# 56 of 96 modulation tiles computed on VectorE as multiply-and-sum over rows, 40 left on TensorE

## The chip, the cores and the metric

The kernel runs on one core of one Trainium2 chip. The time is that of the device for one execution, in microseconds, and a version's time is the median of its runs. Four engines compute: TensorE (PE), VectorE (DVE), ScalarE (ACT) and GpSimd (POOL). SyncE (SP) issues all transfers from memory here, from one queue, in program order.

## The reference, cut to what matters

One latent stream of 256 tokens and a context of 256 tokens, 1024 features each, go through two layers (attention with low-rank queries and keys, then a state-space mixer), each followed by a SwiGLU FFN of width 2816. What the change touches is the modulation: each layer turns two vectors, `c` (latent tokens) and `c_ctx` (context tokens), into 6 x 1024 numbers each.

```python
for i in range(DEPTH):                        # DEPTH = 2
    mod     = silu(c)     @ ada_w[i] + ada_b[i]    # 1024 x 6144, latent
    mod_ctx = silu(c_ctx) @ ada_w[i] + ada_b[i]    # the same weights, context
    shift_a, scale_a, gate_a, shift_m, scale_m, gate_m = split(mod, 6)
    x = x + gate_a * mixer_i(rms_norm(x) * (1 + scale_a) + shift_a)
    x = x + gate_m * ffn_i(rms_norm(x) * (1 + scale_m) + shift_m)
```

So 2 x 6144 output features, each a dot product of length 1024 with either vector. In tiles of 128 output features that is 96 tiles of 128 x 1024 weights, 48 for a layer, 8 for each of the six parts. All of it is float32.

## The kernel before, in words

Tokens lie along the free dimension: 512 for the first layer (256 context, 256 latent), features on partitions. Every large product is made to float32 accuracy from three matmuls on a weight block of 128 x 128: the weights are split into a high part (ACT copies `raw` into `w_hi`, line 537) and a low part (DVE subtracts, line 879), and lines 1324 to 1326 multiply low x high, high x high and high x low. A **weight tile** is 128 x 1024 (eight blocks, 24 matmuls). Four `raw`, `w_hi` and `w_lo` buffers form a ring: tile n+4 can be split once PE is done with tile n. A tile's number starts with `WO` (output projection), `F0` (FFN w1 and w3) or `G0` (FFN w2).

The first FFN runs 22 **rounds** `j`: PE multiplies tile `F0+2j` (w1) and `F0+2j+1` (w3), 48 matmuls over 512 tokens. ACT takes the SiLU of the first product (line 723), splits the next two weight tiles' high parts, and copies the hidden tile's high part (line 727). DVE makes, in this order, the low part of one weight tile, the product of the two halves (line 1090), the low part of the other weight tile, and the low part of the hidden tile (line 1093). Then `w2` runs eight steps `m` of three weight tiles (66 matmuls); PE waits ahead of them for all 22 hidden tiles (`hid_lo`). DVE adds each finished step to the residual with the gate (line 1068), ACT squares it, and POOL sums the squares for the next norm.

The modulation tiles are spread over the program. 16 are multiplied at the start, 32 in the 16 attention heads (two a head) and 48 in the first FFN (two a round, four left over in the first two steps of w2). For a tile, PE runs 8 matmuls of 32 x 128 outputs (line 1359, function `ada`), with the two SiLU vectors as the stationary operand; four of them stand side by side in the array. After four tiles DVE copies the sum out (line 941), PE transposes it back (line 1378, `turn`), and DVE adds the bias (line 946). In the program's order `ada_two` stands behind the FFN round's 48 matmuls, and in a head between the transposes of the probabilities and the next head's scores. PE executes its queue in order, so a modulation tile that has not landed holds up all that follows. The tiles land in two halves of `scratch` (T), by SP's line 281, after SP has issued the weight tiles of the round two later.

Of the kernel before, what the change touches and what calls it, by code (L numbers as in the profile page):

```python
# [76 lines left out]
ADA1 = ADA0 + 2 * HEADS  # L77
# [30 lines left out]
SHARED = (0, 3, 4, 5, 6)  # L108
ODD = [sum(NORM_K[v] // 2 for v in range(w) if v in SHARED) for w in range(len(NORM_K) + 1)]
# [12 lines left out]
def program(nc, a, out):  # L122
# [9 lines left out]
    with ExitStack() as fixed:  # L132
# [103 lines left out]
        ada_used = sem("ada_used")  # L236
        row_cp, row_tr, mod_ev, mod_done = sem("row_copied"), sem("row_turned"), sem("mod_out"), sem("mod_done")
# [30 lines left out]
        def _(sp):  # L268
# [46 lines left out]
            queries(1, 0)  # L315
            sp.wait_ge(nlo, NB[3])
            with sp.Fori(0, 7) as j:
                for u in range(2):
                    queries(2 * j + u + 2, 1 - u)
                    ada_head(2 * j + u)  # L320
            for t in range(8):
                load(WO + t, WO + t, 1024, one("w_o", t))
                if t in (1, 3):
                    ada_head(14 + t // 2)
# [12 lines left out]
            with sp.Fori(1, KH // 2) as i:  # L337
# [5 lines left out]
            for m in range(8):  # L343
                for r, (k0, k1) in enumerate(K3):
                    load(g0(m) + r, g0(m) + r, 128 * (k1 - k0), one("w2", m)[:, 128 * k0:128 * k1])
                    if 3 * m + r in (1, 3, 5, 8):
                        two(KH - 2 + (1, 3, 5, 8).index(3 * m + r))
# [27 lines left out]
        def _(pool):  # L375
# [4 lines left out]
            def accumulate(w, n):  # L380
# [3 lines left out]
                for k in range(1, NORM_K[w] - 1):  # L384
# [3 lines left out]
                    before = T[:, b % 2, 0:n] if k == 1 else T[:, 6, 0:n]  # L388
                    nc.gpsimd.tensor_tensor(T[:, 6, 0:n], before, T[:, (b + k) % 2, 0:n], ADD).then_inc(sq_used, 2 if k == 1 else 1)  # L389
# [45 lines left out]
            pool.wait_ge(ada_used, 96)  # L435
# [90 lines left out]
        def _(act):  # L526
# [184 lines left out]
            head(15, 7, 1)  # L711
            for m in range(8):
# [157 lines left out]
        def _(dve):  # L870
# [78 lines left out]
            def gains(which, layer, chunk, name, groups, k):  # L949

                dve.wait_ge(mod_ev, groups)
# [16 lines left out]
            gains(0, 0, 1, "norm_mix", 4, 1)  # L968
# [57 lines left out]
            def head(i, j, u):  # L1026
# [4 lines left out]
                if u:  # L1031
# [8 lines left out]
                if u:  # L1040
# [19 lines left out]
            gains(1, 0, 4, "norm_ffn", 12, 2)  # L1060
# [18 lines left out]
            def hidden(j, g, u, nt, Uh, Ul, n, s, group=None):  # L1079

                if group is not None:
                    ada_rows(group, 4 * group + 4, bank[7])
                lo(n + 4, s + 4)
                if group is not None:
                    ada_out(group, 1, group - 12)
# [10 lines left out]
            for j in range(2):  # L1096
                hidden(j, j, j % 2, TOK, U0h, U0l, F0 + 2 * j, F0 + 2 * j)
            with dve.Fori(1, KH // 2) as i:
                for u in range(2):
                    hidden(2 * i + u, 2 * i + u, u, TOK, U0h, U0l, F0 + 4 * i + 2 * u, F0 + 2 * u, None if u else 11 + i)  # L1100
            for m in range(8):
                group = {0: 22, 2: 23}.get(m)
                if group:
                    ada_rows(group, 4 * group + 4, bank[7])
                for n in range(g0(m), g0(m + 1)):
                    if n == g0(m) + 2:
                        add(g0(m) + 3, m, m % 2, 0, 5, both)
                    lo(n + RING, n + RING)
                    if n == g0(m) + 1 and group:
                        ada_out(group, 1, group - 12)  # L1110
                if m == 2:
                    gains(2, 1, 1, "norm_mix", 24, 3)
                    gains(3, 1, 4, "norm_ffn", 24, 4)
# [205 lines left out]
        def _(pe):  # L1319
# [8 lines left out]
            def tile(n, s, o, h, l, k0, nk, first, final, mid=None):  # L1328

                pe.wait_ge(w_lo, n + 1)  # L1330
                for k in range(nk):
# [3 lines left out]
                    if k == 3 and mid is not None:  # L1335
                        mid()
# [516 lines left out]
```

## Time and profile before

| | us |
|---|---|
| median of 3 runs | 1361.28 (1359.84 to 1369.13) |
| profiled execution, its own time | 1365.47 |
| its span, first to last instruction | 1363.5 |
| PE busy | 1238.5 (91%) |
| DVE busy | 712.3 (52%) |
| ACT busy | 581.1 (43%) |
| POOL busy | 232.8 (17%) |

PE is busy for most of the span. The mean granted TensorE clock is 0.964 of full speed. The engines' shares are means over stages that differ: start, attention heads (about 112 to 296 us), output projection (to 343), first FFN (353 to 768), state-space mixer, and second FFN, whose tiles carry 256 tokens.

### The profile page before, as it was taken

How to read it: one execution, taken by the hardware profiler on the slowest of the kernel's cores; microseconds unless marked ns; L12 is line 12 of the kernel's file. 1: busy time of each engine (PE TensorE's matmuls, PEld its weight loads, DVE VectorE, ACT ScalarE, POOL GpSimd, SP SyncE). 2: the span in 40 equal slices, each digit the busy share in tenths (PEclk: the TensorE clock that was granted, in tenths of full speed). 3: DMA queues.
4: the chain of work that ended last, by engine and by line, in shares of the span. 5: the costliest groups of instructions: out<-in, count | busy, mean ns of one | idle time of the engine just before them, and what ended most of it. 6: DMA issues, size and time to landing. Idle time of an engine off the chain costs nothing.

```text
span 1363.5 us, 22061 instructions
## 1 busy us (share of the span) xinstructions
PE 1238.5 (91%) x8048; PEld 1010.6 (74%) x8048; DVE 712.3 (52%) x1061; ACT 581.1 (43%) x978; POOL 232.8 (17%) x199
## 2 busy tenths in 40 slices
PE   5797999989599999999999689998988878999997
PEld 3576777768477777777788568888944568999996
DVE  0756666643623323332232566888478765555554
ACT  2545666642522222221222355544543254656542
POOL 0103444423100000000011100001088622000011
PEclk9899999999799999999999899999999879899999
DMA  9203333441244445444333213222600016355562
GB/s 382 98 13 100 124 123 122 148 146 51 107 172 168 150 174 184 155 154 175 117 89 96 77 39 109 78 91 85 197 27 1 0 32 215 125 185 185 177 180 76
DMA packets 50325, 168.03 MB, mean 123 GB/s; under 512 B 5472, under 2 KB 8800, under 8 KB 50144
## 3 DMA queue, kind: packets, MB, share of 16 engines
q1 hardware_dynamic: 50272, 167.32, 36.4%
q8 instruction: 34, 0.56, 0.2%
q14 instruction: 19, 0.16, 0.0%
HBM read 166.25 MB, written 1.05 MB: 123 GB/s over the span
## 4 chain that ended last, share of the span: by engine, by line
PE 68%; DVE 12%; issue 9%; ACT 5%; POOL 4%; DMA 2%; DVEq 0%; SPq 0%; ACTq 0%; POOLq 0%
PE bank L1324 20%; PE bank L1326 20%; PE bank L1325 20%; DVE scratch L1128 4%; PE bank L1359 2%; DVE scratch L1243 2%; PE bank L1690 1%; DMA ada_start<-in_ada_w 1%; PE bank L1678 1%; PE bank L1700 1%; DVE scratch L901 1%; ACT scratch L757 1%; POOL scratch L412 1%; POOL scratch L410 1%; DVE w_lo L879 1%
## 5 line engine op out<-in xcount | busy, mean ns | idle before, releaser
L879 DVE TENSOR_TENSOR w_lo<-raw,w_hi 128x1024 fp32r<-128x1024 f32 (+1 forms) x242 | 282.6, 1175 | 357.1 <-ACT w_hi L537 357.1
L537 ACT ACTIVATE w_hi<-raw 128x1024 fp32r<-128x1024 f32 (+1 forms) x242 | 233.8, 975 | 303.3 <-PE bank L1326 288.6
L1324 PE MATMUL bank<-ffn_h_lo,w_hi 128*128 128x512 f32 (+1 forms) x704 | 244.2, 347 | 14.2 <-DVE ffn_h_lo L916 14.2
L1325 PE MATMUL bank<-ffn_h_hi,w_hi 128*128 128x512 f32 (+1 forms) x704 | 240.6, 342 | 0.0
L1326 PE MATMUL bank<-ffn_h_hi,w_lo 128*128 128x512 f32 (+1 forms) x704 | 240.4, 341 | 0.0
L1324 PEld LDWEIGHTS bank<-ffn_h_lo,w_hi 128*128 128x128 f32 x704 | 134.8, 191 | 35.5 <-issue 19.7
L389 POOL TENSOR_TENSOR scratch<-scratch 128x512 f32<-128x512 f32 (+1 forms) x26 | 40.3, 1551 | 659.2 <-ACT scratch L546 659.2
L1326 PEld LDWEIGHTS bank<-ffn_h_hi,w_lo 128*128 128x128 f32 x704 | 134.7, 191 | 16.6
L1325 PEld LDWEIGHTS bank<-ffn_h_hi,w_hi 128*128 128x128 f32 x704 | 134.7, 191 | 14.9
L1324 PE MATMUL bank<-ssd_h_lo,w_hi 128*128 128x512 f32 (+2 forms) x328 | 116.0, 354 | 12.3 <-DVE ssd_h_lo L916 9.4
L1324 PE MATMUL bank<-ffn_hidden_lo,w_hi 128*128 128x512 f32 (+1 forms) x352 | 120.1, 341 | 4.7 <-DVE ffn_hidden_lo L1093 4.7
L1325 PE MATMUL bank<-ffn_hidden_hi,w_hi 128*128 128x512 f32 (+1 forms) x352 | 119.7, 340 | 0.0
L1326 PE MATMUL bank<-ffn_hidden_hi,w_lo 128*128 128x512 f32 (+1 forms) x352 | 119.6, 340 | 0.0
L1325 PE MATMUL bank<-ssd_h_hi,w_hi 128*128 128x512 f32 (+2 forms) x328 | 114.0, 347 | 0.0
L1326 PE MATMUL bank<-ssd_h_hi,w_lo 128*128 128x512 f32 (+2 forms) x328 | 113.8, 347 | 0.0
L1128 DVE SCALAR_TENSOR_TENSOR scratch<-conv_in,par,scratch 128x512 f32<-128x512 f32 (+1 forms) x96 | 67.9, 707 | 34.8 <-ACT scratch L757 28.1
L1324 PEld LDWEIGHTS bank<-ssd_h_lo,w_hi 128*128 128x128 f32 (+1 forms) x328 | 63.8, 194 | 20.8 <-issue 10.2
L1324 PEld LDWEIGHTS bank<-ffn_hidden_lo,w_hi 128*128 128x128 f32 x352 | 66.6, 189 | 13.8 <-DVE ffn_hidden_lo L1093 5.2
L723 ACT ACTIVATE scratch<-bank 128x512 f32<-128x512 f32 (+1 forms) x44 | 21.6, 491 | 126.2 <-PE bank L1326 126.1
L1326 PEld LDWEIGHTS bank<-ffn_hidden_hi,w_lo 128*128 128x128 f32 x352 | 66.7, 189 | 8.2
L1325 PEld LDWEIGHTS bank<-ffn_hidden_hi,w_hi 128*128 128x128 f32 x352 | 66.5, 189 | 8.0
L1326 PEld LDWEIGHTS bank<-ssd_h_hi,w_lo 128*128 128x128 f32 (+1 forms) x328 | 63.5, 194 | 8.3
(224 smaller groups left out, 2130.7 us busy)
## 6 DMA issues: line engine op xcount, KB each, us to landing
raw<-in_w SPq DMA_DIRECT2D x120, 512.0 KB, 4.3
scratch<-in_ada_w SPq DMA_DIRECT2D x48, 512.0 KB, 4.3
cq<-in_ada_w SPq DMA_DIRECT2D x32, 512.0 KB, 4.3
raw<-in_w_xbc SPq DMA_DIRECT2D x24, 512.0 KB, 3.3
ada_start<-in_ada_w SPq DMA_DIRECT2D x8, 1024.0 KB, 17.3
raw<-in_w_z SPq DMA_DIRECT2D x16, 512.0 KB, 3.6
raw<-in_w_so SPq DMA_DIRECT2D x16, 512.0 KB, 4.4
raw<-in_w SPq DMA_DIRECT2D x16, 384.0 KB, 3.2
```

Source lines behind the costliest of these rows:

```text
L389: nc.gpsimd.tensor_tensor(T[:, 6, 0:n], before, T[:, (b + k) % 2, 0:n], ADD).then_inc(sq_used, 2 if k == 1 else 1)
L410: nc.gpsimd.tensor_tensor(P[:, 1, :], P[:, 1, :], rs_[:, 1:2].to_broadcast([128, 512]), MUL).then_inc(p_norm, 1)
L412: nc.gpsimd.tensor_tensor(P[:, 2, :].rearrange("p (a k) -> p a k", a=2), P[:, 2, :].rearrange("p (a k) -> p a k", a=2), rs_[:, 2:4].unsque ...
L537: A(wh[s % RING][:, 0:c], raw[s % RING][:, 0:c], ACT.Copy).then_inc(w_hi, 1)
L723: A(T[:, u, 0:nt], bank[2 + 2 * u][:, 0:nt], ACT.Silu).then_inc(silu_done, 1)
L879: V.tensor_tensor(wl[s % RING][:, 0:c], raw[s % RING][:, 0:c], wh[s % RING][:, 0:c].bitcast(f32), SUB).then_inc(w_lo, 1)
L1128: V.scalar_tensor_tensor(acc, up[:, u, seg, r:r + 256], par[:, ds(PAR["conv_w"] + 5 * t + r, 1)], acc, MUL, ADD).then_inc(conv_tap, 1)
L1243: last = V.scalar_tensor_tensor(T[:, 2 + h // 4, q], cbf[:, 4 * c + g, :], dt[:, 2 + c, GH * g + h:GH * g + h + 1], T[:, 4 + h // 4, q], M ...
L1324: mm(o, lh, rl, start=first, stop=False)
L1325: mm(o, lh, rh, start=False, stop=False)
L1326: return mm(o, ll, rh, start=False, stop=final)
L1359: last = mm(acc[32 * c:32 * c + 32, 0:128], scm[:, k, :], src[:, at:at + 128], start=k == 0, stop=k == 7)
```

## The change

Tiles 0 to 39 of layer 0 stay on PE: 16 at the start and 24 in heads 0 to 11. Heads 12 to 15, the FFN rounds and w2 have no modulation matmul and no turn. The 56 others (layer 0's last eight, which are the FFN gate, and all 48 of layer 1) are laid out with an output feature per partition, and DVE computes them. Each takes two `scalar_tensor_tensor` instructions of 128 x 1024 (function `matvec`), one for each vector: weights times SiLU row, with the sum over the row written as one number per partition (`accum_out`). Both vectors are loaded as rows repeated on all partitions (`crow`, 1 MB) and put through SiLU by ACT once, behind head 15. Two tiles follow each FFN round on DVE, twelve more come in w2's first six steps. The biases are added in two instructions of their own.

SP waits for `vec_used` (DVE) where it waited for `ada_used` (PE). POOL's accumulator for the norm behind the FFN moves from T[6] to T[3], and POOL waits for `hid_lo` ahead of it.

```diff
-ADA1 = ADA0 + 2 * HEADS
+ADA1 = 40
+VEC = 56
...
-            ada_ffn = [T[:, 4 + 2 * r:6 + 2 * r, :].rearrange("p a n -> p (a n)") for r in range(2)]
+            vec_w = [T[:, 4 + 2 * r:6 + 2 * r, :].rearrange("p a n -> p (a n)") for r in range(2)]
+            crow = sb("silu_c_rows", [128, 2, 1024], f32, ph)
+            vec_prod = sb("matvec_products", [128, 1024], f32, ph)
...
             queries(1, 0)
+            sp.dma_start(crow[:, :, :], a["crow"]).then_inc(crow_in, 16)
             sp.wait_ge(nlo, NB[3])
-            with sp.Fori(0, 7) as j:
+            with sp.Fori(0, 6) as j:
...
             def two(j):
                 for r in range(2):
-                    ada(ADA1 + 2 * j + r, r, ada_ffn)
+                    if late(j, 1):
+                        sp.wait_ge(vec_used, 2 * j + r - 1)
+                    sp.dma_start(vec_w[r], one("vec_w", 2 * j + r)).then_inc(vec_in[r], 16)
...
             head(15, 7, 1)
+            act.wait_ge(crow_in, 16)
+            A(crow[:, :, :], crow[:, :, :], ACT.Silu).then_inc(crow_silu, 1)
...
+            def matvec(v, r, layer, t):
+
+                dve.wait_ge(vec_in[r], 8 * v - 8 * r + 16)
+                if late(v, 1):
+                    dve.wait_ge(vec_out, v)
+                for s, (prod, done) in enumerate(((vec_prod[:, :], vec_out), (vec_w[r], vec_used))):
+                    m = mod[layer][:, ds(t, 1), s:s + 1].rearrange("p t s -> p (t s)")
+                    V.scalar_tensor_tensor(prod, vec_w[r], 1.0, crow[:, s, :], MUL, MUL, accum_out=m).then_inc(done, 1)
+
+            def bias(layer, t0, t1, vectors):
...
-            for j in range(2):
+            dve.wait_ge(crow_silu, 1)
+            for j in range(4):
                 hidden(j, j, j % 2, TOK, U0h, U0l, F0 + 2 * j, F0 + 2 * j)
-            with dve.Fori(1, KH // 2) as i:
+                for r in range(2):
+                    matvec(2 * j + r, r, 0, 40 + 2 * j + r)
+            bias(0, 40, 48, 8)
+            with dve.Fori(2, KH // 2) as i:
                 for u in range(2):
-                    hidden(2 * i + u, 2 * i + u, u, TOK, U0h, U0l, F0 + 4 * i + 2 * u, F0 + 2 * u, None if u else 11 + i)
+                    j = 2 * i + u
+                    hidden(j, j, u, TOK, U0h, U0l, F0 + 4 * i + 2 * u, F0 + 2 * u)
+                    for r in range(2):
+                        matvec(2 * j + r, r, 1, 2 * j + r - 8)
...
-                ada_two(ADA0 + 4 * j + 2 * u, u, ada_mla)
+                ada = not isinstance(i, int) or i < 12
+                if ada:
+                    ada_two(ADA0 + 4 * j + 2 * u, u, ada_mla)
...
             for j in range(2):
                 ffn(j, j, j % 2, TOK, *h0, F0 + 2 * j, F0 + 2 * j, NB[3] if j == 0 else None)
-                ada_two(ADA1 + 2 * j, j, ada_ffn)
```

On PE, at the end of round 1 and the start of round 2, the queue stood so before (`ffn_h` is the FFN's input, `bank` a PSUM bank; the branch opens the loop over rounds):

```order
L1325 MATMUL bank<-ffn_h_hi,w_hi 128x512
L1326 MATMUL bank<-ffn_h_hi,w_lo 128x512
L1359 MATMUL bank<-scratch,silu_c_and_mod_rows 32x128 x16
L1566 UNCONDITIONAL_BRANCH
L1566 ISA
L1330 ISA
L1324 MATMUL bank<-ffn_h_lo,w_hi 128x512
```

and so it stands now (the lines are numbered anew by the change: 1358 to 1360 are the three matmuls):

```order
L1359 MATMUL bank<-ffn_h_hi,w_hi 128x512
L1360 MATMUL bank<-ffn_h_hi,w_lo 128x512
L1598 UNCONDITIONAL_BRANCH
L1598 ISA
L1364 ISA
L1358 MATMUL bank<-ffn_h_lo,w_hi 128x512
```

The block of modulation matmuls between the rounds is gone, and nothing is in its place.

On DVE, the queue of round 0 was this before:

```order
L879 TENSOR_TENSOR w_lo<-raw,w_hi 128x1024
L1090 TENSOR_TENSOR scratch<-bank,scratch 128x512
L879 TENSOR_TENSOR w_lo<-raw,w_hi 128x1024
L1093 TENSOR_TENSOR ffn_hidden_lo<-scratch,ffn_hidden_hi 128x512
L879 TENSOR_TENSOR w_lo<-raw,w_hi 128x1024
```

and is this now (the fifth row there, the next round's first, is the ninth here):

```order
L893 TENSOR_TENSOR w_lo<-raw,w_hi 128x1024
L1116 TENSOR_TENSOR scratch<-bank,scratch 128x512
L893 TENSOR_TENSOR w_lo<-raw,w_hi 128x1024
L1119 TENSOR_TENSOR ffn_hidden_lo<-scratch,ffn_hidden_hi 128x512
L970 SCALAR_TENSOR_TENSOR matvec_products,mod<-scratch,silu_c_rows 128x1024
L970 SCALAR_TENSOR_TENSOR scratch,mod<-scratch,silu_c_rows 128x1024
L970 SCALAR_TENSOR_TENSOR matvec_products,mod<-scratch,silu_c_rows 128x1024
L970 SCALAR_TENSOR_TENSOR scratch,mod<-scratch,silu_c_rows 128x1024
L893 TENSOR_TENSOR w_lo<-raw,w_hi 128x1024
```

Four instructions stand between one round's hidden tile and the next round's weight tile.

## Rows read from the trace of the kernel before

**Rows 1.** The page, part 4: share of the chain that ended last, by engine
```profile
PE 68%; DVE 12%; issue 9%; ACT 5%; POOL 4%; DMA 2%; DVEq 0%; SPq 0%; ACTq 0%; POOLq 0%
```

**Rows 2.** Windows: length, busy PE PEld DVE ACT POOL, PEclk, DMA share, GB/s
```profile
258.00:281.00 23.00, 20.63 (x193) 16.09 (x186) 15.41 (x35) 14.65 (x36) 9.39 (x10) 1.00 0.51 183
...
386.61:636.67 250.06, 250.06 (x1611) 196.10 (x1610) 78.57 (x100) 63.29 (x80) 0.00 (x0) 1.00 0.47 167
366.60:372.80 6.20, 1.91 (x33) 1.00 (x32) 3.58 (x4) 2.87 (x4) 0.00 (x0) 0.86 1.02 402
372.80:377.80 5.00, 5.00 (x16) 3.96 (x13) 0.00 (x0) 0.00 (x0) 0.00 (x0) 0.50 0.93 314
```

**Rows 3.** Timeline of PE in a steady round: start, duration, instruction
```profile
400.92 0.40 PE L1324 MATMUL bank<-ffn_h_lo,w_hi 128*128 128x512 f32 x1
...
411.23 0.40 PE L1326 MATMUL bank<-ffn_h_hi,w_lo 128*128 128x512 f32 x1
...
412.91 0.39 PE L1325 MATMUL bank<-ffn_h_hi,w_hi 128*128 128x512 f32 x1
```

**Rows 4.** Timeline of PE: end of round 0, end of round 1, end of round 21
```profile
366.39 0.39 PE L1326 MATMUL bank<-ffn_h_hi,w_lo 128*128 128x512 f32 x1
370.64 0.73 PE L1359 MATMUL bank<-scratch,silu_c_and_mod_rows 128*32 128x128 f32 x16 [3.85 <-DMA scratch<-in_ada_w]
372.82 0.80 PE L1324 MATMUL bank<-ffn_h_lo,w_hi 128*128 128x512 f32 x1
...
386.22 0.39 PE L1326 MATMUL bank<-ffn_h_hi,w_lo 128*128 128x512 f32 x1
386.54 1.08 PE L1359 MATMUL bank<-scratch,silu_c_and_mod_rows 128*32 128x128 f32 x32
...
636.67 1.08 PE L1359 MATMUL bank<-scratch,silu_c_and_mod_rows 128*32 128x128 f32 x32
```

**Rows 5.** Timeline: from the last FFN round to the first w2 matmul
```profile
639.01 0.68 DVE L1093 TENSOR_TENSOR ffn_hidden_lo<-scratch,ffn_hidden_hi 128x512 f32 x1
...
639.75 0.50 PE L1324 MATMUL bank<-ffn_hidden_lo,w_hi 128*128 128x512 f32 x1 [2.00 <-DVE ffn_hidden_lo L1093]
```

**Rows 6.** Timeline of PE in w2: around a turn, then around two modulation tiles
```profile
652.41 0.39 PE L1326 MATMUL bank<-ffn_hidden_hi,w_lo 128*128 128x512 f32 x1
...
652.99 0.39 PE L1325 MATMUL bank<-ffn_hidden_hi,w_hi 128*128 128x512 f32 x1
...
656.73 0.40 PE L1326 MATMUL bank<-ffn_hidden_hi,w_lo 128*128 128x512 f32 x1
...
658.41 0.39 PE L1325 MATMUL bank<-ffn_hidden_hi,w_hi 128*128 128x512 f32 x1
```

**Rows 7.** Timeline: heads 13 (two rows) and 15
```profile
270.83 0.50 PE L1324 MATMUL bank<-k_lo,q_hi 96*128 96x512 f32 x1 [0.72 <-POOL q_lo L418]
...
273.43 0.36 PE L1324 MATMUL bank<-k_lo,q_hi 96*128 96x256 f32 x1 [0.94 <-DVE silu_c_and_mod_rows L941]
...
291.61 0.60 ACT L682 ACTIVATE probs_t<-bank 128x512 f32<-128x512 f32 x1 [0.28 <-PE bank L1488]
...
293.26 0.66 PE L1500 MATMUL bank<-probs_t,v_head 128*64 128x128 f32 x8
```

**Rows 8.** Instructions by line and form: busy us, mean ns, idle before
```profile
L879 DVE TENSOR_TENSOR w_lo<-raw,w_hi 128x1024 fp32r<-128x1024 f32 x68 | 83.3, 1226 | 206.7 <-ACT w_hi L537 206.7
...
L1128 DVE SCALAR_TENSOR_TENSOR scratch<-conv_in,par,scratch 128x512 f32<-128x512 f32 x80 | 60.2, 752 | 32.0 <-ACT scratch L757 25.8 <-DVE scratch L1128 2.7
...
L1128 DVE SCALAR_TENSOR_TENSOR scratch<-conv_in,par,scratch 128x256 f32<-128x256 f32 x16 | 7.8, 485 | 2.8 <-ACT scratch L757 2.4
```

**Rows 9.** Timeline of ACT: an accumulator's read-out, and its idle time behind head 15
```profile
274.60 0.19 ACT L666 ACTIVATION_READ_ACCUMULATOR scratch<-bank,softmax_negmax 128x1 f32 x1
...
302.15 1.06 ACT L537 ACTIVATE w_hi<-raw 128x1024 fp32r<-128x1024 f32 x1 [6.54 <-PE bank L1326]
```

**Rows 10.** The page, part 6: modulation tiles in the FFN, issue to landing
```profile
scratch<-in_ada_w SPq DMA_DIRECT2D x48, 512.0 KB, 4.3
```

More of the change, by code:

```diff
@@ L108 @@
 SHARED = (0, 3, 4, 5, 6)
+ACC = [6, 6, 6, 6, 3, 6, 6, 6]
 ODD = [sum(NORM_K[v] // 2 for v in range(w) if v in SHARED) for w in range(len(NORM_K) + 1)]
@@ L236, in program @@
         ada_used = sem("ada_used")
+        crow_in, crow_silu, vec_used, vec_out, vec_bias = (sem(x) for x in ("crow_in", "crow_silu", "vec_used", "vec_out", "vec_bias"))
+        vec_in = [sem(f"vec_in{i}") for i in range(2)]
         row_cp, row_tr, mod_ev, mod_done = sem("row_copied"), sem("row_turned"), sem("mod_out"), sem("mod_done")
@@ L320, in _ @@
                     ada_head(2 * j + u)
+            for u in range(2):
+                queries(14 + u, 1 - u)
             for t in range(8):
                 load(WO + t, WO + t, 1024, one("w_o", t))
-                if t in (1, 3):
-                    ada_head(14 + t // 2)
             def both(j, u):
@@ L336, in _ @@
             sp.wait_ge(nlo, NB[4])
-            with sp.Fori(1, KH // 2) as i:
+            for u in range(2):
+                both(2 + u, u)
+                two(u)
+            with sp.Fori(2, KH // 2) as i:
                 for u in range(2):
@@ L967, in _ @@
             ada_out(3, 0, 3)
-            gains(0, 0, 1, "norm_mix", 4, 1)
+            gains(0, 0, 1, "norm_mix", mod_ev, 4, 1)
             both = [(1, 0, CTX), (0, CTX, TOK)]
@@ L1039, in head @@
                     inverse(i + 1, 2)
-                if u:
+                if u and (not isinstance(i, int) or i < 12):
                     ada_out(4 + j, 0, 4 + j)
@@ L1059, in _ @@
             head(15, 7, 1)
-            gains(1, 0, 4, "norm_ffn", 12, 2)
+            gains(1, 0, 4, "norm_ffn", mod_ev, 10, 2)
             def add(used, m, u, layer, chunk, groups):
@@ L1326, in three, with tile @@
                 return mm(o, ll, rh, start=False, stop=final)
-            def tile(n, s, o, h, l, k0, nk, first, final, mid=None):
+            def tile(n, s, o, h, l, k0, nk, first, final):
                 pe.wait_ge(w_lo, n + 1)
@@ L1516, in head @@
                     scores(i + 1, 1)
-                if u:
+                if u and ada:
                     turn_ready(4 + j)
@@ L1520, in head @@
                     scores(i + 1, 2)
-                if u:
+                if u and ada:
                     turn()
@@ L1530, in _ @@
             head(1, 0, 1)
-            with pe.Fori(1, 7) as j:
+            with pe.Fori(1, 6) as j:
                 head(2 * j, j, 0)
                 head(2 * j + 1, j, 1)
+            head(12, 6, 0)
+            head(13, 6, 1)
             head(14, 7, 0)
@@ L1576, in w2 @@
                     tile(n + r, n + r, bank[m % 2][:, 0:nt], h, l, k0, nk, r == 0, r == 2).then_inc(w_used, 1)
-                    if r == 1 and nt == TOK and m in (0, 2):
-                        turn_ready(22 + m // 2)
-                        turn()
             pe.wait_ge(hid_lo, KH)
@@ L1818, in lay_out @@
     o["tab"] = shape_tables()
-    o["ada_w"] = np.concatenate([tiles(w, 512) for w in i["ada_w"]]).reshape(24, 128, 4, 1024).transpose(0, 2, 1, 3).reshape(96, 128, 1024)
+    aw = i["ada_w"][0][:, 0:128 * ADA1]
+    o["ada_w"] = tiles(aw, 512).reshape(ADA1 // 4, 128, 4, 1024).transpose(0, 2, 1, 3).reshape(ADA1, 128, 1024)
+    o["vec_w"] = np.concatenate([i["ada_w"][0].T[128 * ADA1:], i["ada_w"][1].T]).reshape(VEC, 128, 1024)
+    o["crow"] = np.broadcast_to(np.stack([i["c"][0], i["c_ctx"]]), (128, 2, 1024))
     w = i["mla_w_in"][0]
```

59 lines of the change are left out of this document (26 added, 33 removed).

## The prediction

> **What bounds the kernel now.** I read the page's chain of waits first, then the windows of the first FFN, then the timeline of PE at each place where a modulation tile is multiplied, and last the durations of DVE's instructions by form. The chain is PE's for 68% of the span [rows 1]. Over rounds 2 to 21 of the first FFN PE is busy for the whole 250.06 us at a granted clock of 1.00, that is 2.4 GHz, while DVE works 78.57 us and the transfers take 0.47 of the DMA engines [rows 2]. So whatever leaves PE's queue there leaves the time, until DVE becomes as long as PE.
>
> **What it removes in the steady rounds.** Between the third matmul of a round and its last lie 44 spacings, 400.92 to 411.23 us, 0.2343 us each [rows 3]. 48 of them make a round's own work: 11.25 us. From the modulation matmuls of round 1 (386.54) to those of round 21 (636.67) [rows 4] are 250.13 us for 20 rounds, 12.51 us each. The difference, 1.26 us a round, can be seen on the spot: from the last product (411.23) to the second of the next round (412.91) are 1.68 us where two spacings would be 0.47 [rows 3], so 1.21 us for two tiles, and a turn costs 0.11 us in every second round: 652.41 to 652.99 are 0.58 us, again for two spacings [rows 6]. **Saved: 250.13 - 20 x 11.25 = 25.2 us.**
>
> **Round 0.** Its tiles haven't landed when PE comes to them. The last product starts at 366.39, the next round's first at 372.82 [rows 4]: the tiles were issued only when the norm had let go of their buffers, and 402 GB/s were moving [rows 2]. PE then runs for 5 us at a granted clock of 0.50, that is 1.2 GHz, after it had mostly waited for 6.2 us [rows 2]. Without them round 1 starts at 366.39 + 0.23 = 366.62. Its weight tiles were split long before, in the output projection. It ends at 377.87 instead of 386.22 + 0.23 = 386.45. **Saved: 8.6 us.** DVE needs the same late tiles, but only behind round 0's hidden tile, and nobody waits for DVE then.
>
> **Round 21: nothing.** PE waits for the hidden tile's low part, which DVE starts at 639.01, at the end of a chain that starts with PE's last product [rows 5]. The modulation matmuls (1.08 us [rows 4]) lie ahead of the 2.00 us that are left of that wait [rows 5]; without them it is 3.1 us long and emptier, and ends at the same time. DVE's multiplications stand behind the low part, so they don't lengthen it.
>
> **w2.** Two pairs of tiles at 1.21 us (656.73 to 658.41 are again 1.68 us) and two turns at 0.11 [rows 6]. **Saved: 2.6 us.**
>
> **Heads 12 to 15.** In 12, 13 and 14 the modulation matmuls are followed by a wait of 0.7 us for POOL [rows 7]; without them that wait is longer by what they took: nothing. In head 13 PE also waits 0.94 us for the copy of the modulation sums on DVE [rows 7], plus the turn: 1.05 us go. In head 15 the values' product starts at 293.26, behind modulation and turn, while its last input is there at 291.61 + 0.60 = 292.21 [rows 7]: about 0.95 us go. **Saved: 2.0 us**, 0 to 2.5.
>
> **What it adds on DVE.** 112 instructions of 128 x 1024 with a sum. No row shows one. From below: the plain subtraction of this size takes 1.226 us. The nearest rows are the same operation without the sum, 0.752 us for 512 and 0.485 us for 256 elements [rows 8], 1.043 ns an element over 0.218 us, so 1.29 us for 1024. From above, for this case: the 0.19 us by which ACT reads an accumulator out [rows 9], so 1.48 us. I take 1.48. DVE's own work is 78.57 us in 20 rounds [rows 2], of which the ten copies and bias additions of the modulation are little: 3.9 us a round. With four new instructions it is 9.8 us, and PE's round is 11.25. Inside a round DVE falls behind by no more than it catches up: the hidden tile's low part ends 3 us after PE's round (639.69 against 636.6 [rows 4, 5]), the four instructions 6 us later, so the next weight tile's low part, due 7 us after the round (half a round, then ACT's copy), starts 2 us late. PE wants that tile only two rounds on. **Cost: nothing**, covered by DVE's 7.3 us of free time a round. It would cost 21 us for each microsecond a round by which DVE exceeds PE: from (11.25 - 3.9)/4 = 1.84 us an instruction.
>
> In w2 a step is 66 x 0.2343 = 15.5 us of PE. DVE has three low parts (3.7 us), a residual addition (about 1) and the four new instructions (5.9): 10.6 us, covered. The last two steps have none, so the norm behind them doesn't wait. The sums of squares on POOL may shift, to be caught up there too.
>
> **Other queues.** SP now waits for DVE ahead of a modulation tile, and the weight tiles of the round after next but one are queued behind that wait. DVE is done with the buffers about 6 and 9 us into a round; a tile lands in 4.3 us [rows 10], a queue of three in perhaps 6, and ACT wants the weight tile 8 us later. Two megabytes a round in 11.25 instead of 12.51 us raise the DMA share from 0.47 to 0.52: covered. The 1 MB of rows is issued when the transfers pause ahead of the heads. ACT's SiLU of them, twice the size of the 1.06 us copy, and a table load fall into an idle time of 6.54 us [rows 9].
>
> **The sum**: 25.2 + 8.6 + 2.6 + 2.0 = 38.4 us. The profiled execution took 1365.5 us (its span is 1363.5), so it would become 1327.1. It lies 4.2 us above the median of the runs, 1361.3, and I don't know where those 4.2 us are. For the median I forecast **1323 us**.
>
> **A rule against the change.** The rows put the operation with two float32 inputs from SBUF and no sum at 1.043 ns an element, hardly less than the subtraction needs for all its time (1.226 us for 1024, 1.20 ns an element with its fixed part) [rows 8]. The Trainium skill, in "Vector Engine (DVE) Microarchitecture Reference", section "Points that are easy to get wrong", says that this form of instruction with two non-bf16 sources in SBUF runs at half throughput, since no read port is left for the accumulator. The trace disagrees for the form without a sum; no row shows the form with one, and the page's reason is the accumulator. By that rule the sum would be that of rival A.
>
> **Rivals.**
> **A: DVE becomes the bound and the kernel gets slower.** If the sum halves the pace, an instruction takes 0.218 + 2 x 1024 x 0.001043 = 2.35 us, with the read-out 2.54. A round on DVE is then 3.9 + 4 x 2.35 = 13.3 to 14.1 us. Twenty-one rounds take 279 to 296 us, instead of the 270.0 us from 366.62 to the last product's end just ahead of 636.67 [rows 4] (round 0's wait included). Less the 4.6 us of w2 and heads that is +5 to +21: 1366 to 1382 us. It decides from 2.3 us an instruction: (274.6/21 - 3.9)/4. For it speaks only that rule, against it the pace of the same instruction without the sum. Chance 0.07, of which 0.05 beyond 1%.
> **B: the sum costs something in between**, 1.95 to 2.2 us an instruction (a slower drain, or waits of each instruction for the one before). At 2.0 a round is 11.9 us, 21 rounds 14 us more than forecast: 1337 us; the case spans 1333 to 1355. Chance 0.08.
> **C: the clock falls where PE is emptier.** It fell once after a wait like this [rows 2], and half the clock for 5 us cost 2.4 us there. Heads 12 to 15, the output projection's start and w2's start each lose matmuls beside a wait. One to three such falls give 2 to 7 us: 1325 to 1330. Against it: in heads 12 and 13 the granted clock is 1.00 with PE idle for 2.4 of 23 us [rows 2], and 2 us more leave it busy for four fifths. Chance 0.12.
> **D: PE gains more**, since a fall of the clock in the w2 start or a wait in the heads vanishes too: 1313 to 1319. Chance 0.04.
>
> **Numbers.** The forecast itself has 0.68 (1317 to 1328, which holds the bounds of the heads' term and the 4.2 us of unknown place), C 0.12, B 0.08, A 0.07, D 0.04; 0.01 is left for what I don't see. The range for 8 in 10 takes in the forecast and C and the near parts of B and D: 1315 to 1333. What can be told from no change here is about 1%, 13.6 us. Faster by more than that: forecast, C, D and B but for its far end, 0.91. Within it: 0.04, the near end of A and the far one of B. Slower by more: 0.05.
>
> **What would show it.** Rounds 2 to 21 of the first FFN 11.25 us apart on PE, with a granted clock of 1.00 and no wait for DVE: right. PE idle ahead of a round's tile for `w_lo` or `hid_f`, and DVE busy without a gap: A or B, to be read from the mean of the new instruction against 1.84 us. Round 1 directly behind round 0, no 0.50 clock at 373 us: right for the 8.6 us. Products of 0.43 us spacing in heads 12 to 15 or in the output projection: C. The prediction is wrong as a whole if a buffer's release (SP behind `vec_used`) starves the weight ring, which would show as ACT waiting for `raw` in the rounds.

## The result and the profile after

| | before | after |
|---|---|---|
| median of the runs, us | 1363.1 (6 runs, 1359.84 to 1370.21) | **1330.8** (6 runs, 1324.32 to 1333.62) |
| ratio after/before | | **0.9742**, 95% interval 0.9709 to 0.9776 |
| profiled execution, us | 1365.5 (span 1363.5) | 1324.3 (span 1322.5) |

The ratio is 35.2 us saved; the two medians alone differ by 32.3 us, which lies inside the ratio's interval, since the runs of one version spread over some 10 us. The forecast was 38.4 us and 1323 us, with a range of 1315 to 1333. The two profiled executions differ by 41.2 us, more than the medians do, and one of the questions below is where the rest of that comes from. Measured once more, the ratio was 0.9727 (0.9699 to 0.9754).

The page's part 4 of the changed kernel answers to [rows 1]; PE's share of the chain is what it was:

```profile
PE 68%; DVE 11%; issue 10%; POOL 4%; ACT 4%; DMA 1%; DVEq 0%; ACTq 0%; SPq 0%; POOLq 0%
```

Windows of the changed kernel (length, busy PE PEld DVE ACT POOL, PEclk, DMA share, GB/s): the steady rounds, and the stretch behind round 0, to be read against [rows 2].

```profile
376.00:602.00 226.00, 226.00 (x966) 181.71 (x965) 165.85 (x242) 63.33 (x80) 0.00 (x0) 1.00 0.55 188
366.00:372.20 6.20, 6.20 (x28) 4.97 (x27) 4.65 (x7) 3.22 (x5) 0.00 (x0) 1.00 0.97 389
```

PE has no gap in 226 us and runs at a granted clock of 1.00. DVE is now busy for 73% of it, 8.26 us a round of 11.25, where 9.8 were forecast. Behind round 0, where PE had worked 1.91 of 6.20 us, it works all the time, and the 5 us at a clock of 0.50 are gone.

One round on DVE, timeline of the changed kernel (start, duration, instruction, idle time before it and what ended it):

```profile
400.05 0.69 DVE L1116 TENSOR_TENSOR scratch<-bank,scratch 128x512 f32<-128x512 f32 x1 [2.61 <-PE bank L1360]
401.14 1.23 DVE L893 TENSOR_TENSOR w_lo<-raw,w_hi 128x1024 fp32r<-128x1024 f32 x1 [0.40 <-ACT w_hi L549]
402.29 0.68 DVE L1119 TENSOR_TENSOR ffn_hidden_lo<-scratch,ffn_hidden_hi 128x512 fp32r<-128x512 f32 x1
402.89 1.22 DVE L970 SCALAR_TENSOR_TENSOR matvec_products<-scratch,silu_c_rows 128x1024 f32<-128x1024 f32 x1
404.03 0.08 DVE L970 DVE_READ_ACCUMULATOR matvec_products<-scratch,silu_c_rows 128x1 f32 x1
404.03 1.22 DVE L970 SCALAR_TENSOR_TENSOR scratch<-scratch,silu_c_rows 128x1024 f32<-128x1024 f32 x1
...
407.78 1.23 DVE L893 TENSOR_TENSOR w_lo<-raw,w_hi 128x1024 fp32r<-128x1024 f32 x1
411.49 0.69 DVE L1116 TENSOR_TENSOR scratch<-bank,scratch 128x512 f32<-128x512 f32 x1 [2.49 <-PE bank L1360]
```

The low part of the hidden tile comes first, then four multiply-and-sum instructions of 1.22 us that start 1.14 us apart, with their read-outs of 0.08 us in between, then (behind a small bias addition, 0.17 us) the weight's low part; then DVE waits 2.49 us for PE's next round. So PE releases DVE, and not the other way round.

Timeline of PE in the changed kernel, end of round 21, to be read against [rows 5]:

```profile
602.04 0.39 PE L1360 MATMUL bank<-ffn_h_hi,w_lo 128*128 128x512 f32 x1
605.44 0.50 PE L1358 MATMUL bank<-ffn_hidden_lo,w_hi 128*128 128x512 f32 x1 [3.01 <-DVE ffn_hidden_lo L1119]
```

From the last product to w2 are 3.40 us. The wait is 1.01 us longer than the 2.00 of before and ends at the same distance, as the forecast's "round 21: nothing" had it.

**Where the time went, stage by stage.** Each stage ends where PE (in the last two ACT and DVE) starts a certain instruction, read from the timelines. `head 12` is PE's first score product of head 12, behind POOL's `q_lo`; `norm` is ACT's table load for the norm behind w2.

| stage, us | before | before, again | after | after, again |
|---|---|---|---|---|
| start to head 12 | 259.58 | 258.47 | 259.69 | 259.88 |
| head 12 to output projection | 36.60 | 36.59 | 35.92 | 35.91 |
| output projection to first FFN | 57.38 | 57.39 | 57.40 | 57.39 |
| first FFN to its w2 | 286.19 | 284.68 | 252.43 | 252.44 |
| w2 to the norm behind it | 129.81 | 128.26 | 127.19 | 127.19 |
| norm to the last output rows | 587.70 | 590.52 | 583.61 | 586.38 |

Against the first profile of before the change gives 0.7 + 33.8 + 2.6 = 37.1 us, against the second 0.7 + 32.3 + 1.1 = 34.0 us; the ratio's 35.2 lies between. What is left of the 41 us, some 4 us, is in the last row, which the change doesn't touch.

### The profile page after: what moved, and what is told of

It reads as the page before. It is cut to its first block, busy times and chain, and to the rows that moved or that the text cites. A ratio compares the mean times of both kernels' runs of the same rounds, so it can differ in the third digit from the quotient of the medians.

```text
span 1322.5 us, 20410 instructions
## 1 busy us (share of the span) xinstructions
PE 1199.2 (91%) x7138; PEld 986.7 (75%) x7138; DVE 837.5 (63%) x1259; ACT 584.7 (44%) x980; POOL 233.2 (18%) x199
## 3 DMA queue, kind: packets, MB, share of 16 engines
HBM read 167.30 MB, written 1.05 MB: 127 GB/s over the span
## 4 chain that ended last, share of the span: by engine, by line
PE 68%; DVE 11%; issue 10%; POOL 4%; ACT 4%; DMA 1%; DVEq 0%; ACTq 0%; SPq 0%; POOLq 0%
PE bank L1358 21%; PE bank L1359 20%; PE bank L1360 20%; DVE scratch L1162 4%; DVE scratch L1277 2%; PE bank L1716 1%; DMA ada_start<-in_ada_w 1%; POOL scratch L424 1%; POOL scratch L422 1%; PE bank L1704 1%; ACT scratch L771 1%; PE bank L1726 1%; POOL q_lo L430 1%; DVE scratch L915 1%; DVE scratch L898 1%
## 5 line engine op out<-in xcount | busy, mean ns | idle before, releaser
L1358 PE MATMUL bank<-ffn_h_lo,w_hi 128*128 128x512 f32 (+1 forms) x704 | 239.9, 341 | 14.5 <-DVE ffn_h_lo L930 14.5
L970 DVE SCALAR_TENSOR_TENSOR matvec_products<-scratch,silu_c_rows 128x1024 f32<-128x1024 f32 x56 | 73.8, 1317 | 0.0
```

The source lines that it names most:

```text
L970: V.scalar_tensor_tensor(prod, vec_w[r], 1.0, crow[:, s, :], MUL, MUL, accum_out=m).then_inc(done, 1)
L1358: mm(o, lh, rl, start=first, stop=False)
```

## Experiments

All have the changed kernel as their base, except where said; the ratio is to the kernel before, from runs of both on the same chip.

**1. VectorE's new work taken away** (its products are cut to 8 columns, so nearly all of the modulation is left out).

```diff
-V.scalar_tensor_tensor(prod, vec_w[r], 1.0, crow[:, s, :], MUL, MUL, accum_out=m)
+V.scalar_tensor_tensor(prod[:, 0:8], vec_w[r][:, 0:8], 1.0, crow[:, s, 0:8], MUL, MUL, accum_out=m)
```

> The changed kernel, with the 112 multiply-and-sum instructions of VectorE cut from 1024 columns to 8 (this leaves nearly all of the modulation sums of 56 tiles out; the transfers of the weights, the semaphores, SP's order and the number of instructions stay). My theory: VectorE's new work is hidden behind PE everywhere, so taking nearly all of it away changes nothing: the kernel stays at the changed kernel's time, 1331 us within 2 us (0.974 of the kernel before), and PE stays full between 376 and 602 us. The rival: the new work costs something, through VectorE's turns, through the memory that it shares with POOL, or through the weight split that it delays; then this run is faster than the changed kernel by more than 3 us, and the time is missing in the first FFN (rounds, or the 3.4 us between its last product and w2).

Measured: 1329.8 us, ratio 0.9740 (0.9714 to 0.9767), the changed kernel's 0.9742. The window of the steady rounds in this run:

```profile
376.00:602.00 226.00, 226.00 (x966) 181.70 (x965) 85.29 (x242) 63.30 (x80) 0.00 (x0) 1.00 0.54 190
```

DVE works 80.6 us less in this window, and PE's numbers are the same to 0.01 us. First FFN to w2 takes 252.26 us against 252.43, w2 to the norm 127.20 against 127.19. My theory held. The DVE work costs PE nothing in these two stages, and this is shown, not only argued.

**2 and 3. More work on VectorE: six and eight instructions a round instead of four.**

```diff
+for d in range(1):       # range(2) in the second, and 2 * v below
+    m = mod[layer][:, ds(t, 1), d:d + 1].rearrange("p t s -> p (t s)")
+    V.scalar_tensor_tensor(vec_prod[:, :], vec_w[r], 1.0, crow[:, d, :], MUL, MUL, accum_out=m).then_inc(vec_dup, 1)
+    dve.wait_ge(vec_dup, 1 * v + d + 1)
```

> The changed kernel with six multiply-and-sum instructions a round instead of four on VectorE (one of every tile's products is computed once more and then overwritten). In the changed kernel VectorE leaves 2.5 us of a round of 11.25 us free, and one instruction takes 1.15 to 1.22 us. My theory: two more of them, 2.3 to 2.5 us, just fill the round; the time of the rounds stays (0 to 3 us in all, since the last two rounds and w2 may lag a little). The rival of a bound that lies in the latency of the round rather than in its sum (VectorE's low parts come late, PE's tiles wait): some 5 to 25 us more already here.

> The changed kernel with eight multiply-and-sum instructions a round instead of four (both products of each tile computed twice). My theory, VectorE as the longer queue: its round is 3.9 + 8 x 1.15 to 1.22 = 13.1 to 13.7 us against PE's 11.25, so 21 rounds take 39 to 51 us more, and with what w2's steps can't hide 39 to 55 us in all: about the kernel before's time or up to 1.5% above it. This is the case that the forecast's rival A spoke of (an instruction that takes twice as long). The rival, that PE stays the bound because the weights are split two rounds ahead: under 10 us.

Measured with six: 1330.4 us, ratio 0.9732 (0.9691 to 0.9772); first FFN to w2 252.36 us. Window of this run:

```profile
380.00:600.00 220.00, 220.00 (x941) 176.79 (x939) 210.71 (x318) 62.17 (x78) 0.00 (x0) 1.00 0.54 186
```

DVE is 96% busy, and PE still has no gap. So the theory of run 2 held. With eight: 1371.9 us, ratio 1.0054 (1.0032 to 1.0075), 41 us above the changed kernel's median, inside the 39 to 55 us expected; first FFN to w2 297.72 us, 45.3 more. PE's waits from 366 to 652 us in that run (us in total, times, longest), and then two rows of DVE's timeline, a round apart:

```profile
PE bank L1363 <- DVE w_lo L894: 20.8, 15, 1.8
PE bank L1363 <- DVE ffn_hidden_lo L1124: 17.5, 1, 17.5
```

```profile
582.92 1.21 DVE L894 TENSOR_TENSOR w_lo<-raw,w_hi 128x1024 fp32r<-128x1024 f32 x1
...
596.26 1.21 DVE L894 TENSOR_TENSOR w_lo<-raw,w_hi 128x1024 fp32r<-128x1024 f32 x1
```

The round is 13.34 us, DVE's own length, and PE waits for `w_lo`; 21 x (13.34 - 11.25) = 43.9 us. PE's waits in the rounds and the longer wait ahead of w2 (17.5 us, 3.0 before) make up 35.3 of the 45.3 us. The rest isn't idle time: behind such a wait PE can fall to half clock (the mean granted clock from 400 to 622 us is 0.97). The bound changes over between six and eight instructions, and the sum of DVE's instructions puts it there too. The run also stands in for the forecast's rival A: had each of the four instructions taken twice as long, the kernel would have been some 0.5% slower than before.

**4. The wait behind round 0 put back**, without its matmuls.

```diff
+if j == 1:
+    for r in range(2):
+        pe.wait_ge(vec_in[r], 16)
```

> The changed kernel, in which PE waits, between rounds 0 and 1 of the first FFN, until the first two modulation tiles have landed, as the kernel before had to, without multiplying them. It measures the forecast's term for round 0 by itself. My theory: the wait comes back (PE idle for about 5 us after round 0) and behind it the granted clock of 0.50 for about 5 us, which costs 2.4 us: 7 to 8.6 us slower than the changed kernel, 1338 to 1340 us. The rival: the tiles land earlier than in the kernel before, or later work makes up for the wait: 0 to 3 us.

Measured: 1335.0 us, ratio 0.9772 (0.9739 to 0.9805); its interval overlaps the changed kernel's, so the verdict is read from the stages: first FFN to w2 258.20 us, 5.8 more, all other stages up to the norm unchanged. Timeline of PE in this run:

```profile
364.88 0.40 PE L1360 MATMUL bank<-ffn_h_hi,w_lo 128*128 128x512 f32 x1
369.41 0.71 PE L1358 MATMUL bank<-ffn_h_lo,w_hi 128*128 128x512 f32 x1 [4.13 <-issue]
...
372.48 0.58 PE L1359 MATMUL bank<-ffn_h_hi,w_hi 128*128 128x512 f32 x1
372.90 0.39 PE L1360 MATMUL bank<-ffn_h_hi,w_lo 128*128 128x512 f32 x1
```

The step of 4.53 us between the first two rows is 4.30 more than a spacing; then seven spacings of 0.43 us in place of 0.23 and one of 0.51 give some 1.6, 5.9 in all for the 5.8 of the stage. So the mechanism is as forecast (a late tile, then half the clock), and smaller than the expected 7 to 8.6. Against the first profile of before 2.8 us are missing. There the next round starts 6.43 us behind the last product [rows 4], 1.9 more than here, with the modulation matmuls themselves in between, and the half clock lasted 5 us, which makes about 0.9.

**5. The first FFN's part alone.** Heads 12 to 15 keep their eight tiles on PE.

```diff
-ADA1 = 40
-VEC = 56
+ADA1 = 48
+VEC = 48
...
-                ada = not isinstance(i, int) or i < 12
+                ada = True
```

> Only the part of the change in the first FFN: 48 tiles go to VectorE there, and heads 12 to 15 keep their 8 tiles on PE, as in the kernel before. In the changed kernel's profile the granted clock is 0.50 for about 4 us in head 12 and again in head 14, which the kernel before doesn't show. My theory: the falls come from PE being emptier in the four heads, so they are absent here (clock 1.00 from 180 to 300 us); the output projection then starts within 1 us of the changed kernel's 295.6 (relative to its own start of the heads, 0.6 us later), and the total stays within 2 us of the changed kernel: moving the heads' tiles was worth nothing. The forecast's own rival, 2.0 us for the heads: this run 2 us slower than the changed kernel. The rival for the falls, that they vary from execution to execution whatever PE does: they show here too.

Measured: 1326.5 us, ratio 0.9729 (0.9707 to 0.9751). The interval overlaps the changed kernel's (0.9742 and 0.9727): no difference. The medians are 4.4 us apart, but only 1.0 us with the changed kernel's second one, 1327.5. The granted clock stays at 1.00 in the four heads, as expected. Windows of the changed kernel, then of this run:

```profile
260.00:264.00 4.00, 4.00 (x28) 3.53 (x28) 3.32 (x10) 1.80 (x5) 1.34 (x3) 0.67 0.70 228
284.00:288.00 4.00, 4.00 (x24) 3.51 (x25) 3.87 (x8) 2.46 (x6) 0.15 (x1) 0.66 0.52 168
```

```profile
260.00:264.00 4.00, 4.00 (x39) 3.40 (x38) 2.94 (x9) 2.18 (x7) 1.72 (x3) 1.00 1.01 359
284.00:288.00 4.00, 2.92 (x34) 2.42 (x32) 3.83 (x9) 2.10 (x6) 0.87 (x1) 1.00 0.92 347
```

Busy PE looks alike in the first of each pair, but 28 records of matmuls fit in the 4 us instead of 39: at half the clock the same work takes longer and counts as busy. Head 12 to the output projection takes 36.57 us here against 35.92: between these two profiles the heads' part of the change is worth 0.65 us. It isn't even sure: in experiment 1, whose edit doesn't touch the heads, the same stretch took 37.03 us. Where the falls come makes the difference, see below.

**6. PE filled again in heads 12 to 15** (products of an old tile into bank 7, read by nobody).

```diff
+else:
+    if i == 12:
+        pe.wait_ge(mod_ev, 10)
+    for r in range(2):
+        for k in range(4 * u + 2 * r, 4 * u + 2 * r + 2):
+            for c in range(4):
+                at = 512 * (k % 2) + 128 * c
+                mm(bank[7][32 * c:32 * c + 32, 0:128], scm[:, k, :], ada_mla[r][:, at:at + 128], start=k == 0, stop=k == 7)
```

> The changed kernel, with 16 products of the modulation's shape a half-head put back on PE in heads 12 to 15 (they multiply an old tile into bank 7 and nobody reads the result; no transfer, no turn and no copy come back). It tells whether the fall of the granted clock in heads 12 and 14 comes from the missing PE work alone. My theory: yes, the clock stays 1.00 from 180 to 300 us; the two falls cost about 1 to 2 us each, and the filler stands in waits for POOL, so the output projection starts 1 to 3 us earlier than in the changed kernel. The rival, that something else of the change (ACT's SiLU, the 1 MB of rows) lowers it: the falls stay, and the time stays or grows by up to 2 us.

Measured: 1328.4 us, ratio 0.9738 (0.9724 to 0.9753), no difference. Its windows:

```profile
260.00:264.00 4.00, 4.00 (x39) 3.39 (x38) 2.72 (x9) 2.84 (x10) 2.39 (x4) 1.00 0.80 262
284.00:288.00 4.00, 2.00 (x27) 1.52 (x23) 2.75 (x9) 3.20 (x10) 2.75 (x4) 1.00 0.62 221
287.00:292.00 5.00, 3.93 (x46) 2.89 (x48) 1.01 (x3) 2.68 (x7) 1.65 (x2) 0.66 0.01 5
```

The falls in heads 12 and 14 are gone, with ACT's SiLU and the 1 MB of rows still there, so the missing PE work made them. But one fall came in head 15 that the first FFN's part alone doesn't have (it is there in experiment 7 too), and the stage took 36.00 us, so the 1 to 3 us expected didn't come. My theory of the cause holds for two of the falls; that filling helps is not shown.

**7 and 9. Unused products in PE's waits**, first on the kernel of experiment 6, then, with their number cut, on that of experiment 5.

```diff
+def warm(n):
+    for _ in range(n):
+        mm(bank[7][:, :], ones[:, :], tab[:, 0:512], start=True, stop=True)
...
+warm(18)     # ahead of the first FFN; 9 in run 9, which has 5 ahead of the second FFN too
...
+warm(6)      # ahead of its w2; 2 in run 9
...
+warm(18)     # ahead of the state-space projection; 10 in run 9
```

> The filled heads of the run before, and unused products of ones with a table into bank 7 in three of PE's waits: 18 ahead of the first FFN's first round, 6 ahead of its w2, 18 ahead of the state-space projection. In the changed kernel PE starts each of these places at a granted clock of 0.50 (0.43 us from product to product instead of 0.23) for about 4 us. My theory: a PE that isn't empty in the wait keeps or regains a clock of 1.00, which gives back 1.5 to 2.4 us at each of the three places; with the heads 4 to 9 us in all against the changed kernel, 1322 to 1327 us. The rival: the filler outlasts the waits (ones with tab takes 1 us or more each at half the clock) and delays the real work: no gain or up to 10 us slower.

Measured: 1334.6 us, ratio 0.9775 (0.9753 to 0.9797). The rival came true: the filler ahead of the FFN outlasted the wait by 5.6 us. From w2 to the norm this run took 125.95 us, 1.2 less than the changed kernel.

> The first FFN's part of the change alone (heads 12 to 15 keep their tiles on PE), with the unused products cut to what the waits hold: one took 0.87 us in the run with 18, 6 and 18 of them, where the first 18 ended 5.6 us after the wait of 9.3 us would have. So 9 ahead of the first FFN (7.8 us of 9.3), 2 ahead of its w2 (1.7 of 3.0), 10 ahead of the state-space projection (8.7 of 9.4), 5 ahead of the second FFN (4.4 of 4.9). My theory: each place keeps a granted clock of 1.00 and gives back 1.2 to 1.5 us, 4 to 6 us in all against the first FFN's part alone (1326.45 us): 1320 to 1323 us. The rival: a fall of the clock comes anyway in the gap that is left, or later elsewhere, and the time stays at 1326 us within 2 us.

Measured: 1326.0 us, ratio 0.9697 (0.9668 to 0.9727), beside 0.9727 (0.9699 to 0.9754) for the changed kernel beside it (experiment 10). It has the lowest ratio of all versions, but the intervals overlap and the medians are 1.5 us apart. A gain over the changed kernel is therefore not shown, and of the 4 to 6 us that my theory expected against experiment 5 (1326.5 us) nothing is seen: the rival came true. Timeline of PE in run 9, at the first FFN and at w2:

```profile
344.92 7.89 PE L1412 MATMUL bank<-tab,ones 128*128 128x512 f32 x18
354.39 0.48 PE L1355 MATMUL bank<-ffn_h_lo,w_hi 128*128 128x512 f32 x1 [1.58 <-DVE ffn_h_lo L930]
354.70 0.39 PE L1356 MATMUL bank<-ffn_h_hi,w_hi 128*128 128x512 f32 x1
...
358.38 0.50 PE L1355 MATMUL bank<-ffn_h_lo,w_hi 128*128 128x512 f32 x1 [0.96 <-DVE ffn_h_lo L930]
...
606.66 0.50 PE L1355 MATMUL bank<-ffn_hidden_lo,w_hi 128*128 128x512 f32 x1 [1.29 <-DVE ffn_hidden_lo L1119]
607.00 0.40 PE L1356 MATMUL bank<-ffn_hidden_hi,w_hi 128*128 128x512 f32 x1
```

The clock stays up at both places (spacings of 0.23 us from 354.70 on). At the FFN this gives nothing: PE catches up with DVE, which still writes the norm's low parts, and waits 0.96 us at 358.38 and again later; FFN to w2 is 252.27 us, as in experiment 5. At w2 nothing is late next, and w2 to the norm falls from 127.18 to 125.66 us, 1.5 us. So in this run a full clock gave time back at the place where PE is what the others wait for, and none where it wasn't. The last stage, with the two other fillers in it, took 588.14 us against 585.68 in experiment 5, so no gain shows there.

**8. The kernel before, a second time.**

> The kernel before, unchanged, for a second profile. In the first one the granted clock is 1.00 all through 120 to 340 us, and falls to 0.5 in several places of the state-space stage (0.72 at 1080, 0.59 at 1090 us). My theory: heads 12 to 15 show 1.00 again, the places of the falls in the state-space stage differ from the first profile, and the time from the first product of the first FFN to that of its w2 (286.2 us) and on to the norm behind it (129.8 us) is the same within 0.5 us. The rival: the heads' clock varies by itself; then a fall shows here too.

Measured: 1364.1 us. Heads 12 to 15 show 1.00 again, as expected. The FFN and w2 weren't within 0.5 us of the first profile: 1.5 us less each, 284.68 and 128.26. Timeline of PE in this run:

```profile
371.97 0.80 PE L1324 MATMUL bank<-ffn_h_lo,w_hi 128*128 128x512 f32 x1
372.57 0.63 PE L1325 MATMUL bank<-ffn_h_hi,w_hi 128*128 128x512 f32 x1
372.99 0.59 PE L1326 MATMUL bank<-ffn_h_hi,w_lo 128*128 128x512 f32 x1
373.42 0.39 PE L1324 MATMUL bank<-ffn_h_lo,w_hi 128*128 128x512 f32 x1
...
637.13 0.50 PE L1324 MATMUL bank<-ffn_hidden_lo,w_hi 128*128 128x512 f32 x1 [2.00 <-DVE ffn_hidden_lo L1093]
637.47 0.40 PE L1325 MATMUL bank<-ffn_hidden_hi,w_hi 128*128 128x512 f32 x1
637.70 0.40 PE L1326 MATMUL bank<-ffn_hidden_hi,w_lo 128*128 128x512 f32 x1
```

Behind round 0 the clock is back after 1.5 us instead of 5 [rows 2], and behind the wait of 2.00 us ahead of w2 it doesn't fall at all, where in the first profile it fell some 0.8 us into w2. The same program with the same waits gets another clock.

**10. The changed kernel, a second time.**

> The changed kernel, unchanged, on the same chip as the run beside it, for the comparison of the two and a second profile. Expected: 1331 us within 3 us (0.974 of the kernel before); a granted clock of 0.50 in two of the heads 12 to 15, as in all profiles of it and of its variants that leave PE empty there; falls in the state-space stage at places of their own.

Measured: 1327.5 us, ratio 0.9727 (0.9699 to 0.9754). The two falls in the heads and all stages up to the norm are as in the first profile, to 0.01 us, but for 0.2 us at the start; from the norm to the last output rows it is 2.8 us longer. The median lies 3.5 us under the 1331 expected, a little beyond the 3 us that were given it.

## Why the prediction was right, and where its sizes were off

**Steady rounds: right in mechanism and size.** A round takes 11.25 us with PE full. For rounds and round 0 together 33.8 us were forecast; the first profiles differ by 286.19 - 252.43 = 33.76.

**VectorE: right that it costs nothing, and with more room than thought.** The forecast took 1.48 us an instruction, from the 0.19 us in which ACT reads its accumulator. The new line in the changed kernel, first of each tile's two instructions (ns min/median/max; the 56 second ones have a median of 1220):

```profile
L970 DVE SCALAR_TENSOR_TENSOR matvec_products<-scratch,silu_c_rows x56: 1214/1219/2322, 371.0 to 705.7; 128x1024 f32<-128x1024 f32 x56
L970 DVE DVE_READ_ACCUMULATOR matvec_products<-scratch,silu_c_rows x56: 76/82/86, 372.2 to 706.9; - x36, 128x1 f32 x20
```

It is 1.22 us, below my lower estimate of 1.29, with 0.08 us of read-out that lies inside the next spacing. The sum costs no pace: the plain subtraction of that size takes 1.226 us [rows 8]. The rule of rival A, in the Trainium skill's "Vector Engine (DVE) Microarchitecture Reference", "Points that are easy to get wrong", would have made this 2.35 us; the trace disagrees with it, with 1.22 us for two float32 inputs from SBUF and the accumulator in use. The threshold, from which DVE would be the bound, was right too: 1.84 us an instruction for four is 7.4 us of new work a round; six instructions (7.1 us from the first to the end of the last) fitted, eight (9.9 us) made the round 13.34.

**Round 0: right in mechanism, its size holds for one execution.** It was 8.6 us against the first profile. Of these 2.4 us were a half clock that lasted 5 us; in the second profile of before it lasted 1.5 us, and the stage was 1.5 us shorter. So 7.1 to 8.6.

**Round 21 and w2: right, with the same remark.** The wait ahead of w2 grew by what left it. w2 gained 2.62 us against the first profile (forecast 2.6), 1.07 against the second, in which w2 starts at full clock, as the changed kernel's does not. Experiments 7 and 9 put 1.2 to 1.5 us on that half clock; it is one of the places that rival C named.

**Heads 12 to 15: the term that was mis-sized, 0.68 us instead of 2.0.** Timeline of PE in the changed kernel: the score products of heads 12, 13 and 14 behind POOL, and the output projection. The rows of before are in [rows 7] for head 13; the others stood at 259.58, 283.39 and 296.18.

```profile
259.69 0.50 PE L1358 MATMUL bank<-k_lo,q_hi 96*128 96x512 f32 x1 [1.71 <-POOL q_lo L430]
...
272.50 0.50 PE L1358 MATMUL bank<-k_lo,q_hi 96*128 96x512 f32 x1 [1.72 <-POOL q_lo L430]
...
283.81 0.50 PE L1358 MATMUL bank<-k_lo,q_hi 96*128 96x512 f32 x1 [1.72 <-POOL q_lo L430]
...
295.61 0.50 PE L1358 MATMUL bank<-mla_h_lo,w_hi 128*128 128x512 f32 x1 [1.39 <-DVE mla_h_lo L1074]
```

The wait for POOL grew from 0.7 to 1.7 us, as forecast. The steps were 11.25, 12.56 and 12.79 us and are 12.81, 11.31 and 11.80. The second and third are shorter by 1.25 and 0.99, a little over the forecast's 1.05 and 0.95. The first is longer by 1.56, and there the windows shown with experiment 5 have the clock at 0.67 on average. In the run of experiment 1 the first fall came a head later, and there the steps were 11.22, 12.77 and 13.04. So where the first fall doesn't come the step is short, and the fall costs 1.5 us. This is **rival C**, which had 0.12: it came true in the heads beside the forecast, at 1.5 us instead of the 2.4 that I gave it. My argument against it, that PE would still be busy for four fifths of these heads, was true (PE is busy for 27.6 of the 33 us from 257 to 290, the slow stretches counted in) and didn't hold the clock. What the second fall costs depends on its place. In the changed kernel it lies from 285 to 289 us, and the step that holds it is short all the same. In experiment 1 it lies from 293 to 296 us, at the end of head 15, where before had the same 16 products in 1.04 us:

```profile
293.67 1.93 PE L1535 MATMUL bank<-probs_t,v_head 128*64 128x128 f32 x16
296.97 0.50 PE L1358 MATMUL bank<-mla_h_lo,w_hi 128*128 128x512 f32 x1 [1.38 <-DVE mla_h_lo L1074]
```

There the step is 1.2 us longer than the changed kernel's, and the four heads together take 37.03 us, 0.4 more than before the change. So even the 0.68 us hold only for the places that the falls took in five of the six profiles of the changed kernel and of experiments 1 to 4.

**The median.** 1330.8 us lies in the range, 2 us from its end, but above the forecast's own band of 1317 to 1328. Against 1323: 1.3 us are the heads, up to 3.1 the two half clocks that the first profile of before had and the second didn't, 1.8 that the median of before is 1363.1 in these runs and not 1361.3. The rest of the 7.8 us, 1.6 or more, is inside what one median differs from another by: the second one of the changed kernel is 1327.5. These parts are taken from single profiles, so the split is an estimate. The six runs themselves go with their mean granted clock: 1324 and 1325 us at 0.965 and 0.966, 1333 and 1334 us at 0.955. The profiled one is the fastest of them.

**The 4 us of unknown place in the profiled execution** are of the same kind. From the norm behind w2 to the last output rows, where all kernels run the same instructions (but for the unused products of experiments 7 and 9), the twelve profiles of this case take 583.1 to 591.2 us, in no order that goes with the changes (before 587.7 and 590.5, after 583.6 and 586.4). I had seen that one execution lies above the median and could not say where; it is there. The clock goes with it: added up over windows of 5 us, PE's clock in this stage is at half for 57.8 us before and 47.9 us after. Of the ten profiles without unused products there, the six of 583.1 to 586.8 us have 48 to 55 us of it, the four of 587.7 to 591.2 us 58 to 65. Which of PE's waits in the state-space stage meets a fall, and why, stays open.

## What to carry to other kernels

When PE is full, count the work that leaves its queue by the spacing between its instructions, and let the second engine fill up: here it filled 96% of a round without a single gap on PE, and with more work each round was longer by the difference of the two engines' rounds, 2.1 us. Work that leaves a queue beside a wait only lengthens the wait, and can cost clock too: 8 of the 56 moved tiles brought 0.7 us where 2.0 were forecast, in one profile less than nothing, and leaving them where they were changes nothing that can be measured. Before explaining 2 us between two traces of different kernels, take a second trace of one of them.

## What the runs showed of the hardware that was not expected

- **A multiply-and-sum waits for POOL's addition.** Timeline of the changed kernel, in w2, and then of experiment 1, where the instruction has 8 columns instead of 1024:

```profile
640.01 1.72 POOL L401 TENSOR_TENSOR scratch<-scratch 128x512 f32<-128x512 f32 x1 [280.92 <-ACT scratch L558]
640.49 2.32 DVE L970 SCALAR_TENSOR_TENSOR matvec_products<-scratch,silu_c_rows 128x1024 f32<-128x1024 f32 x1
642.74 0.08 DVE L970 DVE_READ_ACCUMULATOR matvec_products<-scratch,silu_c_rows 128x1 f32 x1
642.74 1.22 DVE L970 SCALAR_TENSOR_TENSOR scratch<-scratch,silu_c_rows 128x1024 f32<-128x1024 f32 x1
```

```profile
641.21 1.72 POOL L401 TENSOR_TENSOR scratch<-scratch 128x512 f32<-128x512 f32 x1 [280.76 <-ACT scratch L558]
641.70 1.26 DVE L970 SCALAR_TENSOR_TENSOR matvec_products<-scratch,silu_c_rows 128x8 f32<-128x8 f32 x1
```

  It takes 2.32 us in place of 1.22 while POOL adds two tiles, and the next one, with POOL done, 1.22 again; it is so in five steps of w2. With 8 columns it takes 1.26 us in place of 0.17. So the 1.1 us are a delay, the same for 8 columns as for 1024, and not a slower pace; the one of 8 columns ends 0.03 us behind POOL's instruction. The Trainium skill's "GPSIMD Engine Reference", "1. Specifications", says that the two engines' SBUF access is shared and contends with DVE instructions that have two SBUF inputs; the trace agrees. The forecast had left this out; it cost nothing, since w2's steps had the room (with nearly all of DVE's new work gone, in experiment 1, w2 to the norm takes the same 127.2 us).

- **The granted clock isn't fixed by the program.** With the same 2.00 us of wait ahead of w2 it fell in one execution of the kernel before and not in another (129.81 against 128.26 us). But where the changed kernel leaves PE emptier, in heads 12 to 15, it fell to 0.50 in all of the six profiles taken of it and of experiments 1 to 4 (twice in each, though in experiment 1 at other places), and in none of the four of kernels that keep those tiles on PE (before, twice, and experiments 5 and 9).
